# The swapped half of a rotary embedding: four DMAs per tile against four quarter copies on ScalarE

## The reference, cut to what matters

```python
def rope(t, positions):
    ...
    t1, t2 = t[..., : dim // 2], t[..., dim // 2:]
    rot = jnp.concatenate([-t2, t1], axis=-1)
    return t * cos + rot * sin

def dilated_mixture(q, k, v, positions):
    q = rope(q.reshape(B, S, DIL_HEADS, DIL_HEAD_DIM), positions)
    k = rope(k.reshape(B, S, DIL_HEADS, DIL_HEAD_DIM), positions)
    ...
    for g, (window, dilation) in enumerate(DIL_CONFIGS):
        ... each query sees the keys at m*dilation, |m| <= 64
```

## Time and profile before

| what | value |
|---|---|
| median of three runs | 1714.8 us (1714.66 to 1717.17) |
| profiled execution, its own time | 1715.96 us |
| its span, first to last instruction | 1714.1 us |
| TensorE matmul busy | 1685.5 us, 98% |
| VectorE, ScalarE, GpSimd busy | 745.2, 588.9, 509.1 us |
| TensorE in the dilated stage, 555 to 1160 us | 602.0 us of 605 |
| DMA moved in the whole span | 178.21 MB |

### The profile page before, as it was taken

The page is one execution under the profiler, slowest core; times in us unless marked ns, Lnnn a source line. Parts: engine busy times, 40 slices in busy tenths (PEclk is TensorE's granted clock), DMA queues, the critical chain, the costliest instruction groups (busy, mean ns, idle before and its releaser), DMA issues.

```text
span 1714.1 us, 22710 instructions
## 1 busy us (share of the span) xinstructions
PE 1685.5 (98%) x8753; PEld 1411.7 (82%) x8753; DVE 745.2 (43%) x1486; ACT 588.9 (34%) x1337; POOL 509.1 (30%) x400
## 2 busy tenths in 40 slices
PE   7999999999999999999999999999999999999998
PEld 6778778889878787888978889787787999988886
DVE  4330255334342212344154541535521888855714
ACT  5101456334333103441135310441113777741211
POOL 6125033023333333021220223015313745534310
PEclk9999999999999999999999999999999999999999
DMA  6113012233267422113131222217465535226332
GB/s 205 50 63 109 13 62 70 87 119 94 74 213 270 119 62 59 50 50 85 56 83 38 77 80 58 74 57 265 125 232 160 143 64 139 53 68 212 108 114 98
DMA packets 99293, 178.21 MB, mean 104 GB/s; under 512 B 16201, under 2 KB 36081, under 8 KB 99057
## 3 DMA queue, kind: packets, MB, share of 16 engines
q1 hardware_dynamic: 63280, 95.31, 20.3%
q10 hardware_dynamic: 35904, 81.44, 13.4%
HBM read 115.49 MB, written 48.63 MB: 96 GB/s over the span
## 4 chain that ended last, share of the span: by engine, by line
PE 94%; DVE 2%; DMA 1%; POOL 1%; ACT 1%; issue 0%; SPq 0%; POOLq 0%; DVEq 0%
PE ps L1193 23%; PE ps L1107 14%; PE ps L813 13%; PE ps L1045 5%; PE ps L1360 5%; PE ps L1300 5%; PE ps L1241 4%; PE ps L947 4%; PE ps L1330 4%; PE ps L1313 3%; PE ps L868 3%; PE ps L1209 2%; PE ps L1222 2%; PE ps L999 2%; PE ps L972 1%; PE ps L846 1%
## 5 line engine op out<-in xcount | busy, mean ns | idle before, releaser
L700 POOL TENSOR_SCALAR w_hi<-w_stage 128x1024 fp32r<-128x1024 f32 (+3 forms) x140 | 126.9, 914 | 997.4 <-PE ps L1193 357.0
L707 POOL TENSOR_TENSOR w_lo<-w_stage,w_hi 128x1024 fp32r<-128x1024 f32 (+3 forms) x140 | 270.6, 1941 | 8.9
L1193 PE MATMUL ps<-h2T_hi,w_hi 128*128 128x512 f32 x384 | 156.0, 406 | 0.7 <-ACT gate_tiles L1608 0.7
L1107 PE MATMUL ps<-h2T_hi,w_hi 128*128 128x512 f32 x384 | 154.0, 401 | 0.4 <-issue 0.3
L1193 PE MATMUL ps<-h2T_hi,w_lo 128*128 128x512 f32 x384 | 152.5, 397 | 0.0
L1107 PE MATMUL ps<-h2T_hi,w_lo 128*128 128x512 f32 x384 | 151.6, 395 | 0.0
L1107 PE MATMUL ps<-h2T_lo,w_hi 128*128 128x512 f32 x384 | 151.5, 395 | 0.0
L1193 PE MATMUL ps<-h2T_lo,w_hi 128*128 128x512 f32 x384 | 151.3, 394 | 0.0
L1735 ACT ACTIVATE probs_dil<-probs_dil,dil_stats_out 128x256 f32<-128x256 f32 (+2 forms) x192 | 87.5, 457 | 104.7 <-DVE dil_stats_out L2299 104.7
L1300 PE MATMUL ps<-k_mla,q_mla 128*128 128x512 f32 x384 | 104.3, 407 | 0.0
L2391 DVE TENSOR_REDUCE small<-ps 128x1 f32<-128x1024 f32 x64 | 77.7, 1214 | 55.1 <-PE ps L1300 54.8
(11 more groups left out here) (295 smaller groups left out, 3756.2 us busy)
## 6 DMA issues: line engine op xcount, KB each, us to landing
w_stage<-in_w_in SPq DMA_DIRECT2D x76, 512.0 KB, 3.9
rope_swapped<-rope_in SPq DMA_DIRECT2D x192, 64.0 KB, 2.0
w_stage<-in_w_out SPq DMA_DIRECT2D x16, 512.0 KB, 3.8
gate_scr<-gate_tiles ACTq DMA_DIRECT2D x16, 512.0 KB, 3.7
gates<-gate_scr ACTq DMA_DIRECT2D x32, 256.0 KB, 3.5
dil_scr<-dil_out SPq DMA_DIRECT2D x96, 64.0 KB, 1.6
dil_nums<-dil_scr ACTq DMA_DIRECT2D x24, 256.0 KB, 4.2
x_back<-in_x ACTq DMA_DIRECT2D x8, 512.0 KB, 3.7
```

The source lines that it names most:

```text
L700: last = nc.gpsimd.tensor_scalar(hi_, raw_, 1.0, 0.0, ALU.mult, ALU.add)
L707: last = nc.gpsimd.tensor_tensor(lo_, raw_, hi_.bitcast(F32), ALU.subtract)
L1107: m = pe.matmul(ps[:, gate_bank(u), :], a[:, s, k, P * m_:P * m_ + P], b[:, k, COLS * n:COLS * n + COLS], start=(k == 0 and j == 0), stop= ...
L1193: m = pe.matmul(bank, a, b, start=(k == 0 and i == 0), stop=(k == KT - 1 and i == 2))
```

## The change

ScalarE no longer writes `rope_in`. It makes four copies of 32 rows by 512 columns out of the PSUM bank, each into the swapped quarter of `rope_swapped`, which becomes two buffers of the same total size. The last of the four signals `d_turned`. The 192 DMAs at L606, their waits on SyncE's queue and the waits for them are gone. VectorE's product with the cosine waits for `d_turned`, where it waited for `d_copied`. `d_read` is now signalled by the product with the sine, and the product with the cosine signals `rope_half`. In the slot of a group's first step VectorE does the sine product and the sum before `d_soft`; in other slots they stay behind `d_soft` and `d_out`.

```diff
--- before.py
+++ after.py
@@ -325,8 +325,7 @@
 
     s8 = ExitStack()
     vd = sb("v_dil", [P, TT + 1, COLS], F32, s8)
-    ts = sb("rope_in", [P, COLS], F32, s8)
-    rot = sb("rope_swapped", [P, COLS], F32, s8)
+    rot = sb("rope_swapped", [P, 2, COLS], F32, s8)
     osb = sb("dil_out", [P, 2, G, HD], F32, s8)
     dstat = sb("dil_stats_out", [P, 2, TT, STAT], F32, s8)
     masks = sb("masks", [P, MASK_W + P], F32, s8)
@@ -595,15 +594,6 @@
         def load_chunks(first, end):
             for n in range(first, end):
                 load_chunk(n)
-
-        def swap_halves(u):
-
-            r = rope_units(u)
-            sp.wait_ge(*after("d_copied", r + 1))
-            if r:
-                sp.wait_ge(*after("roped", r))
-            for b in range(4):
-                sp.dma_start(rot[32 * b:32 * b + 32, :], ts[32 * (b ^ 1):32 * (b ^ 1) + 32, :]).then_inc(sem("swapped"), 16)
 
         def d_rows(g, t):
             start, step = tile_start(g, t)
@@ -669,9 +659,6 @@
             u = slot // 2
             if slot % 2 == 0 and u in panel_start:
                 place, start = slot, panel_start[u]
-            done = unit_before(slot)
-            if done and done[3] != "v":
-                swap_halves(done[0])
             if slot - 2 in step_at:
                 g, i = step_at[slot - 2]
                 d_store(g, i)
@@ -1747,18 +1734,22 @@
             done = unit_before(slot)
             if done:
                 u, r, g, kind, t = done
-                if kind == "v" and t == 0:
-                    act.wait_ge(*after("d_read", u))
-                    if g:
-                        act.wait_ge(*after("d_valued", d_step(g, 0)))
-                act.wait_ge(*after("d_done", u + 1))
                 if kind == "v":
+                    if t == 0:
+                        act.wait_ge(*after("d_read", u))
+                        if g:
+                            act.wait_ge(*after("d_valued", d_step(g, 0)))
+                    act.wait_ge(*after("d_done", u + 1))
                     act.activation(vd[:, t, :], ps[:, d_bank(u), :], ACT.Copy).then_inc(sem("d_read"), 1)
                 else:
-                    if r:
-                        act.wait_ge(*after("swapped", 64 * r))
-                    act.activation(ts[:], ps[:, d_bank(u), :], ACT.Copy,
-                                   scale=HD ** -0.5 if kind == "q" else 1.0).then_inc(sem("d_copied"), 1)
+                    act.wait_ge(*after("d_done", u + 1))
+                    if r >= 2:
+                        act.wait_ge(*after("roped", r - 1))
+                    for b in range(4):
+                        out_rows, rows = slice(32 * b, 32 * b + 32), slice(32 * (b ^ 1), 32 * (b ^ 1) + 32)
+                        last = act.activation(rot[out_rows, r % 2, :], ps[rows, d_bank(u), :], ACT.Copy,
+                                              scale=HD ** -0.5 if kind == "q" else 1.0)
+                    last.then_inc(sem("d_turned"), 1)
             if slot in step_at:
                 d_exp(*step_at[slot])
             if slot == D_SLOTS - 2:
@@ -2270,19 +2261,17 @@
                 dve.wait_ge(*after("d_scored", d_step(g - 1, 4 * j + 4)))
             if kind == "q" and (g or j >= 2):
                 dve.wait_ge(*after("d_scored", d_step(g, 4 * (j - 2) + 4)))
-            dve.wait_ge(*after("d_copied", r + 1))
+            dve.wait_ge(*after("d_turned", r + 1))
             nc.vector.scalar_tensor_tensor(rope_dst(g, kind, t), grouped(g, n, ps[:, d_bank(u), :]), HD ** -0.5 if kind == "q" else 1.0,
-                                           grouped(g, n, cosT[:, COLS * n:COLS * n + COLS]), ALU.mult, ALU.mult).then_inc(sem("d_read"), 1)
+                                           grouped(g, n, cosT[:, COLS * n:COLS * n + COLS]), ALU.mult, ALU.mult).then_inc(sem("rope_half"), 1)
 
         def rope_sin(u, r, g, kind, t):
-
             n = t % 2
-            dve.wait_ge(*after("swapped", 64 * (r + 1)))
-            nc.vector.tensor_tensor(rot[:], rot[:], sinT[:, COLS * n:COLS * n + COLS], ALU.mult).then_inc(sem("rope_half"), 1)
+            nc.vector.tensor_tensor(rot[:, r % 2, :], rot[:, r % 2, :], sinT[:, COLS * n:COLS * n + COLS], ALU.mult).then_inc(sem("d_read"), 1)
             dve.wait_ge(*after("rope_half", r + 1))
             dve.wait_ge(*after("d_read", u + 1))
             dst = rope_dst(g, kind, t)
-            nc.vector.tensor_tensor(dst, dst, grouped(g, n, rot[:]), ALU.add).then_inc(sem("roped"), 1)
+            nc.vector.tensor_tensor(dst, dst, grouped(g, n, rot[:, r % 2, :]), ALU.add).then_inc(sem("roped"), 1)
 
         def d_soft(g, i):
             n = d_step(g, i)
@@ -2311,14 +2300,17 @@
             done = unit_before(slot)
             rope = done and done[3] != "v"
             if rope:
-                if done[4] == 0 and done[3] == "q":
-                    dve.wait_ge(*after("d_read", done[0]))
                 rope_cos(*done)
+            first = slot in step_at and step_at[slot][1] == 0
+            if rope and first:
+                rope_sin(*done)
             if slot in step_at:
                 d_soft(*step_at[slot])
             if slot - 2 in step_at:
                 d_out(*step_at[slot - 2])
-            if rope:
+            if rope and not first:
+                if done[4] == 0 and done[3] == "q":
+                    dve.wait_ge(*after("d_read", done[0]))
                 rope_sin(*done)
             if slot == D_SLOTS - 2:
                 group_stats = [stats[:, 0], stats[:, 1], dstat[:, 0]]
```

## The result

The median of eight runs went from 1714.92 to **1721.14 us**; the ratio is 1.0034, with a 95% interval of 1.0026 to 1.0043. Forecast were 1716.5 us and no measurable change, in a range up to 1719.5. The medians lie 6.2 us apart and the spans of the two profiled executions 5.4; what the traces can explain is the 5.4, since executions of one kernel scatter by 2.5 to 4 us. Nearly all of it is in the dilated stage. I measure this stage in each trace from the start of its first projection matmul to the start of the last product with the values; the trace gives both as the first and last start of a line. Before it is 1156.34 - 558.88 = 597.5 us, after 1161.45 - 558.78 = 602.7: **+5.2 us**. Stage lengths are rounded to 0.1 us, and differences are taken before rounding.

The account below looks back on a forecast made before the run. TensorE, busy 1685.5 of 1714.1 us, was taken as the bound, so only its waits count. Group one 0, group two 0.8 and group three 0.9 made +1.7 us: median 1714.8 becomes 1716.5 us, range 1714.0 to 1719.5.

Parts of the forecast that it names:

- What bounds the kernel, and the path: TensorE bounds; added copies could delay its next scores through cosine product and row maxima, by latency, not ScalarE load.
- the removal of the DMAs: Group three's first step: without the wait for the swap, scores 2 can start 0.3 us earlier.
- The length of the four copies: ScalarE: each added copy costs 0.49 us, so the signal to VectorE comes 1.47 us later; outer end 2.25.
- Steady slots: Later even slots: chain from copies to scores fits, 4.71 us against 4.92 in group three; cost 0.
- Step 3 of each group: Delay of the scores after step 2: 0 in group one, 0.8 us in group two, 0.9 in group three.
- The first slot: Sine product and sum before a group's first maxima: groups one and two 0, with up to 0.25 us lost.
- Rival A: Quarter copies don't overlap: at 0.75 us each, steady slots of group three stall too; 1721.1 us, chance 0.14.
- Rivals B and C: B: chain has more room, 1714.3 us, chance 0.12. C: late rotation holds a PSUM bank, 1740 us, chance 0.02.
- the mild end of A: VectorE's quarter rule carried over to ScalarE: some 0.60 us a copy and 1718 us.

Follow-up runs that it names:

- run 5: Changed kernel with one 128-row copy for the four (halves not swapped), first slot's sine product and sum behind the maxima: 1714.97 us, stage 597.1.
- run 1: Changed kernel with each of the four quarter copies writing the rows it reads (halves not swapped): 1719.36 us, ratio 1.0020.
- run 2: Changed kernel with all four copies from rows 32-63 to rows 0-31, each of another 128 columns: 1715.33 us, stage 598.1.
- run 4: Changed kernel with the sine product and sum of each group's first slot put back behind the row maxima: 1721.54 us, stage 601.8.
- run 3: Changed kernel with one 128-row copy in place of the four (halves not swapped): 1716.36 us, ratio 1.0003, stage 597.8.
- run 9: Kernel before, DMAs kept, with every step's scores behind the slot's projection matmuls; run twice: ratios 0.9984 and 0.9986, stage 595.4 us.

## Why the prediction was wrong, step by step

**What bounds the kernel, and the path.** Right. The loss is on the path named: copies, cosine product, maxima, next scores, with TensorE's work unchanged. I gave the removal of the DMAs 0.3 us, and run 5 found 0.3, in the same place.

**The length of the four copies: the step that failed.** "The signal to VectorE comes 3 x 0.49 = 1.47 us later than now." The measured delay, in the third group from a unit copy's start to the cosine product, went from 0.68 us (1081.97 to 1082.65 in the trace before) to 2.50 (1084.30 to 1086.80): 1.82 later. The copies also start 0.14 later behind the transposes' copy, which I had not counted at all. Together 1.96 for 1.47. For the same reason ScalarE's added load was 88 us (588.9 to 676.9) where I had 71. The row behind the 0.49 was of two copies in the same quarter, and runs 1 and 2 show that this is exactly the case in which they overlap. I had named the doubt and kept it as a bound, but I took the row for the likeliest value although the copies differ from it in the property that counts. The rule that the Trainium skill states for VectorE ("VectorE: DVE Perf Modes", Two Vector instructions with no wait between them) described it: an instruction that starts in another 32-row quarter than the last one is held until the earlier ones have finished. The traces show the same on ScalarE: in all 48 units of the changed kernel the copies start 0.60 us apart, each 0.01 after the end of the one ahead.

**Steady slots: "cost 0".** Wrong by the size alone. 4.71 + 0.49 = 5.20 us against a slot of 4.92 gives 0.28 a slot; measured were 1.2 us in four, 0.30 each. The working stands, with 0.2 us of room and a price that was off by 0.5. Groups one and two have no repeated stall, as said.

**Step 3 of each group.** Forecast 0, 0.8 and 0.9, measured 0.3, 2.1 and 1.5. The 0.5 us of the copies accounts for most of the miss in groups one and three. In group two it leaves 0.8. With 1.96 in place of 1.47 the prediction's own working gives 0.3 + 1.3 + 1.4 for these places and 1.1 for the steady slots, 4.1 us; with the next term, 0.8, it is 4.9 of the 5.2 measured.

**The first slot: "0, with up to 0.25 lost".** Too little. Putting the sine product and the sum ahead of the first maxima cost 0.8 us with four copies (run 4 against the change) and 0.7 with one (run 5 against run 3). In group two VectorE's timeline shows it: the sine product took 1.38 us beside GpSimd's split, and the first maxima started at 873.06, where they had started at 870.70 before; the scores of step 1 then waited until 874.57.

```profile
869.57 1.08 DVE L2265 SCALAR_TENSOR_TENSOR qT_dil<-ps,cos_table_T 128x512 f32<-128x512 f32 x1 [0.43 <-ACT rope_swapped L1750]
870.56 1.38 DVE L2270 TENSOR_TENSOR rope_swapped<-rope_swapped,sin_table_T 128x512 f32<-128x512 f32 x1
...
873.06 0.42 DVE L2288 CUSTOM_DVE_ANT_0 probs_dil<-ps,masks 128x256 f32<-128x256 f32 x1
```

I had also called the 1.6 us between scores 1 and 2 a stall; 0.6 of it was (the wait at that place in group one, 0.8 in group three), and run 9 shows the difference.

**Rivals.** Rival A, "the quarter copies don't overlap", is what happened. Its time, 1721.1 us, matches the measured 1721.14 partly by chance: it was worked out with 0.75 us a copy, and at the true 0.60 the same text gave 1718. The remainder is mostly the gap ahead of the first copy and the first slot's order; 1.0 us of the 6.2 between the medians is not in the stage at all. Rivals B and C are out; no wait for a bank appeared.

**The range.** It ended at 1719.5, so the mild end of A, 1718, was inside. What carried the time out of it was that three terms went the same way: the spacing, the gap ahead of the first copy, and the first slot. The stage alone, 5.2 us on 1714.8, gives 1720.0.

Group two's 0.8 us are the reordering: run 4 undoes it, and 0.75 go. Why it costs there and not elsewhere is argued only. In the first slot of groups one and three the same order makes scores 1 wait nowhere. In group two the wait ahead of scores 1 is 0.67 us, and the sine product is longer by 0.69: 1.38 us while GpSimd's last low part runs (3.09 us for 2.38 before), 0.69 in run 4, where it starts behind that part. No run moved the split.

## What to carry to other kernels

When one instruction is cut into pieces on other rows, price the pieces from rows in which consecutive instructions also change their quarter; the back-to-back overlap of about 0.1 us is lost at every change, and at the neighbours ahead and behind too. A transfer that shows up in other engines' idle time may be free for the bounding engine, and its replacement lands on an instruction stream whose place in the order decides the price: four copies that took the same 2.39 us gave a stage 5.2 us longer than the kernel before, 1.0 longer, or 0.8 longer than run 9, which has its scores in the same late place. And a wait list's idle time is the figure for what a reordering can give, not the gap between two starts of one line.

## What the runs showed of the hardware that I had not expected

On ScalarE, a copy that reads another 32-row quarter than the instruction ahead does not overlap it, whether or not it also writes another. With 512 columns the spacing is 0.60 us at a change of quarter (the changed kernel and run 1) and 0.49 without one. With 128 columns in one quarter, the overlap is 0.095 us (run 2). A change on the reading side alone is enough: in run 2 the first copy writes quarter 0 behind a writer of quarter 0, reads quarter 1, and starts 0.62 after a 0.60 us instruction. A change on the writing side alone was in no run. Writing 32 rows away from where one reads costs nothing measurable: a copy takes 590 ns in the changed kernel and 588 in run 1.
